# Hybrid decoder step: who multiplies the norm factor into the ConvFFN's hidden tile

## The reference

```python
def conv_ffn(h, st, w_in, wc, w_down):
    z = h @ w_in
    g, st_new = causal_dwconv(z[..., :D_FF], st, wc)
    return (jax.nn.silu(g) * z[..., D_FF:]) @ w_down, st_new

hp = hp + conv_ffn(rms_norm(hp, g_ffn[layer]), zf, w_ffn_in[layer], conv_f_w[layer], w_down[layer])[0]
```

## Time and profile before

| what | value |
| --- | --- |
| median of 3 runs | 2599.93 us (2598.96 to 2603.32) |
| the profiled execution's own time | 2608.27 us |
| its span, first to last instruction | 2606.5 us |
| mean granted TensorE clock | 0.991 of full speed |
| GpSimd busy, instructions | 968.2 us, 635 |
| VectorE busy, instructions | 1655.7 us, 2593 |
| ScalarE busy, instructions | 802.5 us, 1402 |
| in-product stage of layer 0, layer 1 | about 370 to 853 us, about 1843 to 2326 us |

### The profile page before, as it was taken

The page is one execution under the profiler, slowest core; times in us unless marked ns, Lnnn a source line. Parts: engine busy times, 40 slices in busy tenths (PEclk is TensorE's granted clock), DMA queues, the critical chain, the costliest instruction groups (busy, mean ns, idle before and its releaser), DMA issues.

```text
span 2606.5 us, 41678 instructions
## 1 busy us (share of the span) xinstructions
PE 2531.8 (97%) x17036; PEld 2375.7 (91%) x17036; DVE 1655.7 (64%) x2593; ACT 802.5 (31%) x1402; POOL 968.2 (37%) x635
## 2 busy tenths in 40 slices
PE   8999998999999999999999999989899999999997
PEld 8999988999999999987777777759899999999997
DVE  6999777666666555655555555564766666665555
ACT  5111343333333211333333333343433333331112
POOL 1000126777777322321010101124277777752222
PEclk9999999999999999999999999999999999999998
DMA  4111102455444544444444444433077778775321
GB/s 152 41 41 41 44 17 66 141 141 143 145 139 160 194 163 146 172 147 146 143 148 147 141 167 146 165 108 121 25 267 267 269 273 291 267 276 183 99 83 67
DMA packets 106557, 383.93 MB, mean 147 GB/s; under 512 B 23936, under 2 KB 41216, under 8 KB 103936
## 3 DMA queue, kind: packets, MB, share of 16 engines
q1 hardware_dynamic: 106368, 381.26, 43.3%
HBM read 339.15 MB, written 176.04 MB: 198 GB/s over the span
## 4 chain that ended last, share of the span: by engine, by line
PE 89%; DVE 7%; issue 2%; ACT 1%; DMA 1%; POOL 0%; DVEq 0%; SPq 0%; ACTq 0%
PE reg L949 29%; PE reg L808 20%; PE reg L775 12%; PE reg L1061 9%; PE ob L949 3%; PE reg L1041 3%; PE ob L1097 3%; PE reg L881 2%; PE reg L1014 1%; PE reg L1082 1%; PE ob L1082 1%; PE reg L1150 1%; PE reg L1137 1%; DVE neg_s L2299 1%; DMA w_raw<-in_wstream 1%
## 5 line engine op out<-in xcount | busy, mean ns | idle before, releaser
L949 PE MATMUL reg<-xo,wq 128*128 128x352 f32 x5280 | 862.6, 324 | 24.7 <-ACT part L1288 11.5
L949 PEld LDWEIGHTS reg<-xo,wq 128*128 128x128 f32 x5280 | 852.4, 189 | 28.2 <-ACT part L1288 12.1
L808 PE MATMUL reg<-hid,w_sp 128*128 128x352 f32 x3150 | 509.0, 323 | 0.0
L808 PEld LDWEIGHTS reg<-hid,w_sp 128*128 128x128 f32 x3150 | 508.7, 188 | 0.0
L488 POOL TENSOR_TENSOR w_sp<-w_raw,w_sp 128x1024 fp32r<-128x1024 f32 x63 | 173.9, 2763 | 739.3 <-ACT w_sp L483 718.8
L1837 DVE TENSOR_TENSOR h<-reg,h 128x1056 f32<-128x1056 f32 x199 | 250.1, 1257 | 274.1 <-PE reg L808 226.7
L775 PE MATMUL reg<-xs,w_sp 128*128 128x352 f32 x2016 | 332.5, 326 | 10.2 <-DVE xs L1826 9.8
L775 PEld LDWEIGHTS reg<-xs,w_sp 128*128 128x128 f32 x2016 | 328.1, 189 | 13.6 <-issue 13.1
L1714 POOL TENSOR_TENSOR wq<-wqr,wq 128x512 fp32r<-128x512 f32 x168 | 235.1, 1410 | 164.6 <-DVE wqr L2066 164.6
L1714 POOL TENSOR_TENSOR wq<-w_raw,wq 128x512 fp32r<-128x512 f32 x168 | 255.5, 1531 | 94.9 <-ACT wq L1275 94.8
L1061 PE MATMUL reg<-xs,w_sp 128*128 128x352 f32 x1512 | 279.6, 332 | 0.4 <-DVE VT L2281 0.4
(11 more groups left out here) (249 smaller groups left out, 2946.3 us busy)
## 6 DMA issues: line engine op xcount, KB each, us to landing
w_raw<-in_wstream SPq DMA_DIRECT2D x192, 512.0 KB, 4.3
out_sv<-in_cache_v SPq DMA_DIRECT2D x16, 4088.0 KB, 16.7
out_sk<-in_cache_k SPq DMA_DIRECT2D x16, 4088.0 KB, 16.8
kvr<-in_kva SPq DMA_DIRECT2D x16, 2048.0 KB, 9.1
kvr<-in_kvb SPq DMA_DIRECT2D x16, 1536.0 KB, 6.9
hid_spill<-tmp SPq DMA_DIRECT2D x44, 528.0 KB, 5.4
hraw<-hid_spill SPq DMA_DIRECT2D x44, 528.0 KB, 4.5
wt<-in_wtab SPq DMA_DIRECT2D x16, 512.0 KB, 4.4
```

Source lines behind the costliest of these rows:

```text
L808: mm = nc.tensor.matmul(out[:, t, :], w[:, wh, kk * 512 + m * P:kk * 512 + (m + 1) * P], hid[:, par_g, kk, xh, t * TS:(t + 1) * TS], start ...
L949: mm = nc.tensor.matmul(out, w[:, wh, k * P:(k + 1) * P], xo[:, o, 1 - xh if o == X_T3 else xh, k, :], start=(first and k == 0 and wh + xh ...
```

## The change

GpSimd no longer multiplies `sil` by `rst`. VectorE's `hidden(j)` waits for the SiLU itself (`silu_ok`), makes the three products from the unscaled `sil`, waits for the completion of the third (`chain`, which adds a semaphore count and a wait on it) and of the first two (`prod_ok`), and then multiplies the whole tile `tmp` (128x1056) by `rst` in place. The third count of `prod_ok` now comes from this multiplication. The semaphore `silr_ok` is no longer used.

```diff
@@ GpSimd, ffn @@
-                def silu_scale(j):
-                    pool.wait_ge(silu_ok, NJ * L + j + 1)
-                    nc.gpsimd.tensor_tensor(sil[:, PAD:], sil[:, PAD:], rst[:, :], ALU.mult).then_inc(silr_ok, 1)
-
...
                 for j in range(NJ):
-                    if j > 1:
-                        silu_scale(j - 1)
                     if j > 0:
                         quad_lo(L, j, Q_S3)
                         quad_lo(L, j, Q_A22)
-                    if j == 1:
-                        silu_scale(0)
                     if j < NJ - 1:
...
                     else:
                         split_lo(pool, down_unit(L, 0, 0))
                         history(j)
-                        silu_scale(j)
                         split_lo(pool, down_unit(L, 0, 1))
                         split_lo(pool, down_unit(L, 1, 0))
@@ VectorE, hidden(j) @@
                     jj = J0 + j
-                    dve.wait_ge(silr_ok, jj + 1)
+                    dve.wait_ge(silu_ok, jj + 1)
...
                     for t, u in up:
-                        nc.vector.tensor_tensor(third(tmp, t), u, third(sil[:, PAD:], t), ALU.mult).then_inc(prod_ok, 1)
+                        ins = nc.vector.tensor_tensor(third(tmp, t), u, third(sil[:, PAD:], t), ALU.mult)
+                        if t == 1:
+                            chain(ins)
+                        else:
+                            ins.then_inc(prod_ok, 1)
+                    dve.wait_ge(prod_ok, 3 * jj + 2)
+                    nc.vector.tensor_tensor(tmp[:, :], tmp[:, :], rst[:, :], ALU.mult).then_inc(prod_ok, 1)
```

## The result

The changed kernel is slower by a quarter of a per cent. Over 20 runs of each its median is 2610.05 us (2606.06 to 2621.4) and that of the kernel before 2604.45 us (2598.96 to 2610.19); the ratio is 1.0026 with a 95% interval of 1.0016 to 1.0036, so 4 to 9 us. It lies above the stated range, on the side of rival C, the only one that lay beyond that range there, with 4 chances in 100. The kernel before itself came out 4.5 us above the median of the three runs shown, which explains a part of the distance in absolute numbers but nothing of the ratio.

The account below looks back on a forecast made before the run. TensorE, busy 97% of the span, was taken to bound the kernel. Terms -0.4 and +0.5 us summed to +0.1 us, carried over from the median 2599.93 to 2600.0 us; range 2595.5 to 2605.5.

Parts of the forecast that it names:

- rival C: Late rounds: a GpSimd subtraction falls before gate scaling L2114, the 0.84 us cover goes; +19 us, 2619 us; chance 0.04.
- TensorE bounds, and VectorE's 178.3 us of idle time are worth nothing: In-product stage: removing VectorE's 40 waits for GpSimd, 178.3 us, only moves idle time to its wait for TensorE.
- rival D: In-product rounds: VectorE's freed 4.46 us per round make the kernel faster, the whole 178.3 us giving 2422 us; chance 0.03.
- The round's sum: Late round: SiLU wait, three products and a 2.25 us multiplication end at 695.9 us, at most 696.5; price in 42 rounds nothing.
- The work behind the multiplication on GpSimd's queue, moved earlier: Late round: GpSimd's subtractions at 695.05 and 696.30 come up to 2.06 us earlier; price nothing.
- The rule of the Trainium skill: Speaks against the added VectorE multiplication, which contends with GpSimd; the round was to absorb even the longer value.
- The last tile of each layer: Between two down-projection additions: new multiplication takes 1.25 us, costs nothing; at 2.84 us it would cost 0.9 us, twice.
- The start of layer 1: Second layer's start: multiplication before the taps against GpSimd's lead, between -0.6 and +2.84, taken +0.2; with cache copy +0.5 us.
- the term for the cache copy: Second layer's start: the copy starts 1.3 us later, so the weight load overlaps more of it; 0 to +1.3, taken +0.3.
- The 0.4 us of layer 0: First layer: TensorE's one wait behind 440 us, behind a load sharing DMA engines with a cache copy, counted as gone; -0.4 us.
- GpSimd's busy time down by 90 us: Sign of being right: GpSimd loses 44 multiplications of 2.054 us each, 90 us of its busy time.
- late waits for L2106: Sign of being wrong: TensorE waits for VectorE's sum at L2106 in the late rounds.

Follow-up runs that it names:

- the version with the early low parts: Changed kernel with both GpSimd waits put back and the low parts of round 1's S3 and A22 made ahead of round 0's history copy; 2601.78 us, ratio 0.9987.

## Why the prediction was wrong

- **TensorE bounds, and VectorE's 178.3 us of idle time are worth nothing**: right. No late round changed, and rival D (faster through the freed 4.46 us) got nothing.
- **The round's sum**: right. Taken 2.25 us for the multiplication, measured 2.234; first combination forecast at 695.9, measured 695.63 on the same scale. The upper bound of 2.84 us was never reached.
- **The work behind the multiplication on GpSimd's queue, moved earlier ("TensorE is not waiting for them, so their price is nothing")**: this is the step that failed. It was true of those that wait for them, and asked nothing about what they run beside. I looked at who needs the moved instruction, and not at whom it disturbs, and only in a late round. What the runs showed in its place: the moved subtractions hold up VectorE at the end of each in-product stage, and TensorE waits 2.0 us there, 4.1 us in all; with GpSimd made to wait again the ratio falls from 1.0042 to 1.0007, and with no new VectorE instruction at all it is still 1.0025.
- **The rule of the Trainium skill** (GPSIMD Engine Reference, Key points: the SBUF interfaces are shared, with contention against VectorE instructions with two SBUF inputs) was put to the new instruction alone. By the same words it applied to those that the freed GpSimd work now met, the hidden tile's low part and the two later taps, which have two SBUF inputs as well. The trace agrees: 3.44 instead of 1.25 us, 4.63 instead of 2.60 us.
- **The last tile of each layer ("The new instruction has no GpSimd work beside it")**: right for that instruction (1.26 us, TensorE not kept waiting), and it was the wrong instruction to look at. The GpSimd multiplication removed at this place was a gate for two subtractions of 2.4 us, over 20 us ahead of the tile. Missed: 4.1 us.
- **The start of layer 1**: GpSimd's lead was counted as a gain only. It was one at the taps of round 1 (the first took 0.74 instead of 1.78 us, the pair 2.60 instead of 3.51), and TensorE's wait for L2106 fell from 2.1 to 1.4 us where 2.6 was taken, though the second profiles have 2.4 before and 2.3 after. But the same lead reached the taps of round 0 and delayed VectorE by 0.9 us. And the term for the cache copy, taken at +0.3 us, was 1.4: counted from VectorE's reciprocal the copy was issued 1.4 us later, and the load on the chain took 11.79 instead of 10.35 us. In layer 0 I had said that the change can't reach the wait in round 1, since "no product tile is made before it". A product tile isn't; GpSimd's next subtraction is. Missed: 0.9 us of VectorE's time in each layer, of which between nothing and 1.6 us reached TensorE in all. The 0.4 us of layer 0 were gone, as taken.
- **GpSimd's busy time down by 90 us**: it fell by 58.3, since one group of its subtractions is held up by 40 us beside the new instruction.
- **The rivals**: C had the right kind of mechanism, one more subtraction of GpSimd in front of a VectorE instruction, at the wrong place. It was bound to the rounds, where the subtractions are in fact tied to TensorE.
- **The number itself**: 2600.0 was carried over from a median of three runs that lay low; of the 20 runs of before the median is 2604.45. The range had 1 us for drift on the slow side, too little beside steps of 3.3 us that differ from layer to layer and execution to execution. Even so, 2599.9 us with the measured ratio would be 2606.7, above the range: the miss is not the drift's alone.
- **What should have shown it wrong** (late waits for L2106) did not, and did not cover what happened: the list looked for the failure only where the argument had looked.

## What to carry to other kernels

An instruction that waits also holds back what is queued behind it, and taking it away releases that work to wherever it can run: follow each released instruction to the stretch where it lands and read what the engine that it can hold up does there, at the start and the end of a loop above all. If an order protects something, keep it by a wait that says so rather than by an instruction that happens to wait. And before a difference of a few tenths of a per cent is explained from two profiles, check that the stretches that the change does not touch run at the same pace in both.

## What the runs showed of the hardware

- A VectorE instruction that meets a running GpSimd subtraction ended about its own time after that one ended: the low part that takes 1.25 us began at 853.66, GpSimd's subtraction ended at 853.60 + 2.39 = 855.99, and the low part at 857.10. The same with the second of the pair of taps of round 0 in layer 1 of the changed kernel: the first took 1.30 us, the second began at 1889.88, beside a subtraction from 1889.87 to 1891.13, and ended at 1892.21. Both read as if the two had taken turns rather than shared.
- VectorE's reciprocal of 128x1024 took 6.54 us with GpSimd subtracting beside it (at 409.64 us in the version with the early low parts) and 6.55 us with GpSimd idle (at 1124.02 in the kernel before), and the early subtractions beside it took 1.3 us, near their shortest (1.26).
- TensorE's pace in one and the same stage took one of three values, 0.7% apart, at granted clock 1.00, as told above.
